# Three norms' column sums: GpSimd adds seven tiles of squares, TensorE multiplies two tiles with ones in place of eight

## The reference, cut to what matters

```python
def rms_norm(x, g):
    xf = x.astype(F32)
    y = xf * lax.rsqrt(jnp.mean(xf * xf, axis=-1, keepdims=True) + EPS)
    return (y * g.astype(F32)).astype(x.dtype)

x = x + rms_norm(mix, mix_norm_post[l])
h = rms_norm(x, mem_norm_pre[l])                       # input of the memory attention
x = x + rms_norm(memory_attention(h, m, ...), mem_norm_post[l])
h = rms_norm(x, ffn_norm_pre[l])                       # input of the up projection
x = x + rms_norm(conv_ffn(h, ...), ffn_norm_post[l])
...
u = _rmsnorm(h, norm_w[i])                             # i = 0: input of the convolution
h = h + _short_conv_mixer(u, conv_in_w[j], conv_w[j], conv_out_w[j])
```

## Time and profile before

| what | value |
|---|---|
| median of 3 runs | 925.24 us (925.12 to 925.93) |
| the profiled execution, its own time | 926.31 us |
| its span (first to last instruction) | 924.6 us |
| PE busy | 911.6 us (99% of the span) |
| PEld busy | 856.3 us (93%) |
| DVE busy | 657.1 us (71%) |
| ACT busy | 533.1 us (58%) |
| POOL busy | 129.5 us (14%) |
| mean granted TensorE clock | 1.000 |

### The profile page before, as it was taken

How to read it: one execution, slowest core, us unless ns; L and a number is a source line. 1 busy time by engine, 2 the same in 40 slices (tenths; PEclk the granted TensorE clock), 3 DMA queues, 4 the chain that set the end, 5 groups by cost and what they waited for, 6 DMA issues and landing times.

```text
span 924.6 us, 19102 instructions
## 1 busy us (share of the span) xinstructions
PE 911.6 (99%) x6977; PEld 856.3 (93%) x6977; DVE 657.1 (71%) x1116; ACT 533.1 (58%) x905; POOL 129.5 (14%) x122
## 2 busy tenths in 40 slices
PE   8999999999999999999999999999999999999997
PEld 7997899998999999889999999999999998888886
DVE  4898877555899997447877777766577566767743
ACT  6767677445776676446444444444454567666643
POOL 2210011000055666000111111101010000000000
PEclk9999999999999999999999999999999999999999
DMA  8752425535356665762655555565465544454561
GB/s 298 260 187 97 155 93 167 174 115 179 124 169 192 200 205 179 229 188 97 196 174 175 176 178 172 175 198 178 142 199 178 170 145 142 159 170 160 182 198 52
DMA packets 45075, 157.91 MB, mean 171 GB/s; under 512 B 6067, under 2 KB 7219, under 8 KB 44764
## 3 DMA queue, kind: packets, MB, share of 16 engines
q1 hardware_dynamic: 44524, 155.56, 51.3%
q0 software_dynamic: 496, 1.59, 0.6%
HBM read 156.06 MB, written 1.06 MB: 170 GB/s over the span
## 4 chain that ended last, share of the span: by engine, by line
PE 93%; DVE 3%; ACT 2%; issue 1%; DMA 1%; SPq 0%; DVEq 0%; ACTq 0%
PE acc L1300 13%; PE acc L1302 13%; PE acc L1301 13%; PE scores L1300 6%; PE scores L1301 5%; PE scores L1302 5%; PE acc L1253 4%; PE acc L1255 4%; PE acc L1254 4%; PE scores L1255 2%; PE scores L1253 2%; PE scores L1254 2%; PE outs L1253 2%; PE outs L1255 2%; PE outs L1254 2%; PE acc L1375 1%
## 5 line engine op out<-in xcount | busy, mean ns | idle before, releaser
L1859 DVE TENSOR_TENSOR w_lo<-raw,w_hi 128x1024 fp32r<-128x1024 f32 x288 | 356.1, 1243 | 98.1 <-ACT w_hi L652 97.6
L652 ACT ACTIVATE w_hi<-raw 128x1024 fp32r<-128x1024 f32 x288 | 302.2, 1056 | 150.4 <-PE acc L1302 64.8
L1300 PE MATMUL acc<-XH,w_hi 128*128 128x256 f32 (+1 forms) x624 | 178.2, 286 | 1.4 <-DVE SQ L2171 1.1
L1301 PE MATMUL acc<-XL,w_hi 128*128 128x256 f32 (+1 forms) x624 | 175.8, 282 | 0.0
L1302 PE MATMUL acc<-XH,w_lo 128*128 128x256 f32 (+1 forms) x624 | 175.8, 282 | 0.0
L1300 PEld LDWEIGHTS acc<-XH,w_hi 128*128 128x128 f32 x624 | 117.4, 188 | 3.9 <-issue 2.1
L1300 PE MATMUL scores<-XH,w_hi 128*128 128x272 f32 (+1 forms) x424 | 120.2, 283 | 0.0
L1301 PE MATMUL scores<-XL,w_hi 128*128 128x272 f32 (+1 forms) x424 | 119.7, 282 | 0.0
L1302 PE MATMUL scores<-XH,w_lo 128*128 128x272 f32 (+1 forms) x424 | 119.7, 282 | 0.0
L1301 PEld LDWEIGHTS acc<-XL,w_hi 128*128 128x128 f32 x624 | 117.5, 188 | 0.1
L1302 PEld LDWEIGHTS acc<-XH,w_lo 128*128 128x128 f32 x624 | 117.4, 188 | 0.0
(11 more groups left out here) (533 smaller groups left out, 1797.1 us busy)
## 6 DMA issues: line engine op xcount, KB each, us to landing
raw<-weights SPq DMA_DIRECT2D x288, 512.0 KB, 3.6
cst<-params SPq DMA_DIRECT2D x1, 1080.5 KB, 8.8
XR<-x_t SPq DMA_DIRECT2D x2, 512.0 KB, 6.4
Y<-mem_t SPq DMA_DIRECT2D x1, 1024.0 KB, 7.6
AR<-bias_rows POOLq DMA_DIRECT2D x4, 256.0 KB, 6.4
out<-AR SPq DMA_DIRECT2D x2, 512.0 KB, 2.7
AR<-final_gain POOLq DMA_DIRECT2D x1, 512.0 KB, 7.5
cst<-params SPq DMA_DIRECT2D x1, 114.5 KB, 3.6
```

The costliest lines, as they stand in the source:

```text
L652: nc.scalar.activation(w_hi[:, n % SLOTS, :], raw[:, n % SLOTS, :], ACT.Copy).then_inc(hi_ready, 1)
L1300: nc.tensor.matmul(o, wh, h, start=start, stop=False)
L1301: nc.tensor.matmul(o, wh, l, start=False, stop=False)
L1859: V.tensor_tensor(w_lo[:, s, :], raw[:, s, :], w_hi[:, s, :].bitcast(F32), ALU.subtract).then_inc(lo_ready, 1)
```

## The change

Three calls of `stat_x` become calls of `stat_sum`, and GpSimd's program gets three more calls of `sum_squares`: two behind the one of the mixer's norm, and one ahead of the convolution's loop. The count that the mLSTM's norm waits for goes from 2 to 5.

```diff
             sum_squares(lambda m: wait_evacuated(pool, TILE["w_out"] + m), META)
+            for count in (1, 2):
+                sum_squares(lambda m: pool.wait_ge(sq_ready, KT * count + m + 1), META)
...
+            sum_squares(lambda m: pool.wait_ge(sq_ready, KT * 3 + m + 1), 0)
             with pool.Fori(0, E_TILES) as i:
                 pool.wait_ge(c_conv, i + 1)
...
-            stat_x(NORM_X1, 1, S)
+            stat_sum(NORM_X1, 2, lambda: pe.wait_ge(sq_ready, 2 * KT), S)
...
             side_by_side(3, CHUNK["up"], TILE["up"], up_acc, xh, xl, RAW_X2)
-            stat_x(NORM_X2, 2, S)
+            stat_sum(NORM_X2, 3, lambda: pe.wait_ge(sq_ready, 3 * KT), S)
...
             side_by_side(3, CHUNK["conv_in"], TILE["conv_in"], conv_acc, xha, xla, RAW_H0)
-            stat_x(NORM_H0, 3, T)
+            stat_sum(NORM_H0, 4, lambda: pe.wait_ge(sq_ready, 4 * KT), T)
...
             chunk(CHUNK["lgates"], TILE["lgates"], xha, xla, T, ready=raw_ready(RAW_H1))
-            stat_sum(NORM_H1, 2, lambda: pe.wait_ge(sq_ready, SQ_H1 + KT), T)
+            stat_sum(NORM_H1, 5, lambda: pe.wait_ge(sq_ready, SQ_H1 + KT), T)
```

## The result

The changed kernel takes 932.1 us (median of 6, 930.63 to 933.5) beside 925.75 us before in the same comparison: ratio 1.0067, 95% interval 1.0056 to 1.0077, 6.3 us slower. The forecast was 926.3 us and "within 0.2%", with a range up to 928.7. The profiled execution has a span of 931.8 us, 7.2 us more than before.

The account below looks back on a forecast made before the run. The prediction took TensorE, busy 99% of the span, to bound the kernel. Its terms, +2.4 at X1 and -0.67 each at X2 and H0, gave +1.06 us on the median 925.24, so 926.3 us, range 923.9 to 928.7.

Parts of the forecast that it names:

- TensorE as the bound, and 0.67 us a norm: Whole kernel: TensorE is busy 99% of the span; 8 products for 32 save 0.67 us per norm if it never waits.
- Exclusion of GpSimd and VectorE, X1 step by step: At X1, GpSimd additions and VectorE operations with two SBUF inputs exclude each other; query chunk 2.4 us later, 0.67 counted.
- the walk: Addition-by-addition timing at X1: first ends at 152.15, third at 154.9, sixth at 160.65; TensorE stands still some 3 us.
- The cover at X2 and H0: `side_by_side` leaves 2.96 and 3.4 us for the additions; TensorE does not wait and gains 0.67 us at each.
- The delays of `XL` and `w_lo`: Rival, chance 0.18: VectorE's late work reaches TensorE at X2 and H0, or X1 fares worse; 927.6 or 928.7 us.
- the slack for the `w_lo`: At X2, the fourth chunk's `w_lo` would be done at about 243.2, 0.7 us before it is needed.
- The clock: Rival, chance 0.12: a 3 us stop at X1 drops TensorE to 1.2 GHz; one chunk costs 2.8 us more, 929.1 us.
- the 1.1 us wait: TensorE's longest wait before the change, apart from the start; the clock stayed at 2.4 GHz behind it, cited against the rival.
- decides from a stop of somewhere over 1.1 us: The 0.12 rival's condition at X1: the stop length from which the clock would fall to the lower level.
- the prediction's own signs of being wrong: X1 wait under 1 or over 4 us; `XL` or `w_lo` wait in or behind `side_by_side`; clock falling behind X1.
- A product taken from TensorE is time gained: Whole kernel: products removed gain and TensorE stops lose time one for one, since nothing else could absorb either.
- the forecast's part (1.06): Sum over the three norms: 2.4 us lost at X1, 0.67 gained at X2 and at H0, +1.06 us.

## Why the prediction was wrong

- **TensorE as the bound, and 0.67 us a norm**: right. 0.67 us was gained at X2 and 0.71 at H0.
- **Exclusion of GpSimd and VectorE, X1 step by step**: right, with the three ends of additions that the rows give within 0.05 us of the walk. X1's step is 2.61 us, of which 0.21 are the clock's, and 2.38 to 2.40 in the four profiled executions whose sums were made at the full clock; 2.4 was forecast. The Trainium skill's sentence (GPSIMD Engine Reference, Key points: shared SBUF interfaces, contention with instructions of two SBUF inputs) is borne out by `XL` at 0.96 us for 0.48.
- **The cover at X2 and H0**: right. No wait; GpSimd's last addition at X2 ended at 246.90 in the changed trace, 1.1 us before TensorE's sums at 247.97, where the prediction had 1.4 (242.1 and 243.52). The delays of `XL` and `w_lo` did not reach TensorE, but the slack for the `w_lo` was 0.35 us, half of the 0.7 that was forecast.
- **The clock**: this is the first step that failed. I had it as a rival at 0.12 and 2.8 us; it is worth 2.45 us at the query chunk and 0.21 at the sums in the profiled run, and about 0 to 2.7 us over the runs. My argument against it, that the clock had stayed behind the 1.1 us wait, said nothing about a stop of 3 us. The forecast held the stop of 3 us and the unchanged clock at once, and no row showed that these go together. Nor is it so that the clock "decides from a stop of somewhere over 1.1 us": three executions of the experiments have it at 0.50 behind waits of 0.30 to 0.84 us among small products, so the length of a stop alone doesn't tell. Of the prediction's own signs of being wrong, this one came: the granted clock fell behind X1. The Trainium skill (TensorE: Matmul & The Clock Gate, What's actually happening) makes the throttled clock the default that activity lifts; the trace agrees, 0.50 from 160 to 166 us. With the stop at 1.1 us, or filled with small products, the clock stayed at 1.00.
- **"A product taken from TensorE is time gained"**: the second step that failed, and the larger one, 4.4 us in the loop. It took a product's price to be a constant of its shape. The price is 0.113 or 0.118 us for the same 256-column product, clock and neighbours, for hundreds of products. The up loop was quick in the kernel before and slow with X2's new form (all nine runs of that kernel at 928.57 us or more). The sum had no such term, nor did the range. It could have been seen before: the starts in `side_by_side` are 0.118 us apart and those in the loop 0.113.
- **The numbers**, for the two profiled executions: 2.40 - 0.67 - 0.71 is 1.0 us, the forecast's part (1.06); the clock's 2.66 makes it 3.7 and the loop's 4.38 makes it 8.1, less 0.5 by the two `side_by_side` and 0.33 up to X1: 7.2 us.

What stays open: why there are two paces, and what picks one. The kernel before isn't free of it either: beside these runs it took 930.03 us once in 18 and 927.56 to 928.02 four times in 33, and no trace says by what. The number of small products fits in eight of eight cases for most runs, but not in all runs, and not when a product is shortened or where a pause falls in the loop. No other engine was tried as the cause, and an experiment that moves the loop's start by time alone, without another product, was not made. That the unprofiled runs 4 us apart differ in the pace is argued from the profiled ones.

## What to carry to other kernels

A chained sum on a second engine costs its whole tail where the first engine used to follow the data tile by tile: at the place itself it pays where a long stretch of other products covers the tail (X2, H0: 0.7 us each) and not where the next instruction is already at the door (X1: 2.4 us). Put a stop of TensorE into the sum with the clock it may cost, and look for rows of a stop as long before holding the clock for granted. When a change of a few hundred nanoseconds moves a kernel by several microseconds, count the products in a fixed window of an untouched loop before and after; if the count differs with no wait, try one small product more or less ahead of the loop.

## What the runs showed that I had not expected

- 256-column products start 0.113 or 0.118 us apart in stretches of hundreds, at a granted clock of 1.00 and without waits (709 and 682 products in 80 us). One small product of some 0.2 us ahead of the loop moved the kernel before by 4.3 us (two in place of one), and leaving the one out moved it by 4.6.
- When a GpSimd addition and a `w_lo` both wait, the order was the one of the walk: GpSimd ahead of VectorE's next operation if it waits when the current one ends, and VectorE ahead of GpSimd's next addition (157.11, 1.75 us for 1.22: `w_lo` let one addition go first, not two).
- The clock fell behind a stop of 3.0 us in all four kernels profiled with it; the windows show it at half from 160 us on in one and from 162 us in another, so that the cost differs from run to run (928.2 to 930.5 us for the same kernel). It also fell at 57 us in three executions, ahead of everything that was changed, at a cost of some 1.5 us.
